# Attention queries stored head by head in full 128-row tiles with zeros, in a two-block float32 model kernel

## The reference

```python
# block 1, heads of 64
h = rms_norm(x, mix_norm_g);  proj = h @ w_in          # 1024 x 8708
# four mixers, 4 heads each: stick breaking (sb), dilated (dil, 3 groups), forgetting (fox), differential (diff)
sb:   z = q k^T / 8, log-sigmoids and a suffix sum over keys, then exp, times v
dil:  s_g = q_g k_g^T / 8 - slope * distance, softmax over the 3 groups together, times v_g
fox:  softmax(q k^T / 8 + cum_q - cum_k), times v
diff: w = softmax(q_0 k_0^T / sqrt(32) - slope*dist) - lam * softmax(q_1 k_1^T / sqrt(32) - slope*dist), w v
      # q_0, q_1, k_0, k_1: two halves of 32 of one head of 64
x = x + (sum_n sigmoid(gate_n) * (y_n @ w_branch_n)) @ w_out
x = x + relu(rms_norm(x) @ w_up)**2 @ w_down;  x = rms_norm(x, final_norm_g)
# block 2: 8 heads of 64 with q/k norm and rotary (one block of 256 keys, so plain causal attention),
# beside a gated causal convolution of 31 taps with a layer norm; then w_out, then a gated MLP
```

## Time and profile before

| what | value |
|---|---|
| median of 3 runs | 833.12 us (832.48 to 836.74) |
| the profiled execution: its time, its span | 833.48 us, 831.6 us |
| PE busy | 801.0 us, 96% of the span |
| PEld, DVE, ACT, POOL busy | 659.9, 470.7, 405.2, 34.6 us |
| share of PE in the chain that ended last | 85% |
| granted TensorE clock | 0.999 of full speed |
| HBM read | 134.43 MB, 163 GB/s over the span |

### The profile page before, as it was taken

One profiled execution on the slowest core, in us unless ns is written; L12 is line 12 of the kernel. 1 busy time (PEld: TensorE's weight loads), 2 busy tenths in 40 slices (PEclk: granted clock), 3 DMA queues, 4 the chain that ended last, 5 costly groups with the idle time before them and its releaser, 6 DMA issues.

```text
span 831.6 us, 9701 instructions
## 1 busy us (share of the span) xinstructions
PE 801.0 (96%) x3930; PEld 659.9 (79%) x3930; DVE 470.7 (57%) x616; ACT 405.2 (49%) x539; POOL 34.6 (4%) x33
## 2 busy tenths in 40 slices
PE   5999999999999999999999999898999999999997
PEld 4877888877778778788888877776887788888896
DVE  5454444556666767544544536688965745445443
ACT  5555444445555744654454454745446544343340
POOL 0000000000001320000000003011000000000000
PEclk9999999999999999999999999999999999999999
DMA  9832333343445445655555562935113655545341
GB/s 341 290 131 99 126 102 133 121 152 107 148 153 177 156 141 204 217 203 173 180 196 167 194 202 72 384 109 202 52 51 102 238 168 198 193 166 201 101 153 50
DMA packets 68268, 136.25 MB, mean 164 GB/s; under 512 B 2304, under 2 KB 7040, under 8 KB 67584
## 3 DMA queue, kind: packets, MB, share of 16 engines
q1 hardware_dynamic: 67760, 134.44, 47.3%
q10 hardware_dynamic: 464, 1.20, 0.4%
HBM read 134.43 MB, written 1.05 MB: 163 GB/s over the span
## 4 chain that ended last, share of the span: by engine, by line
PE 85%; DVE 7%; ACT 3%; issue 2%; DMA 1%; POOL 1%; ACTq 0%; SPq 0%; DVEq 0%
PE b L542 19%; PE b L544 18%; PE b L543 18%; PE SS L542 4%; PE SS L544 4%; PE SS L543 4%; PE TT L511 3%; DVE wlo L1407 3%; PE OO L542 2%; PE OO L544 2%; PE OO L543 2%; PE OO L850 2%; ACT whi L1009 1%; PE SS L627 1%; PE b L686 1%
## 5 line engine op out<-in xcount | busy, mean ns | idle before, releaser
L1407 DVE TENSOR_TENSOR wlo<-raw,whi 128x2048 fp32r<-128x2048 f32 (+2 forms) x123 | 273.8, 2228 | 169.4 <-ACT whi L1009 169.3
L1009 ACT CAST whi<-raw 128x2048 fp32r<-128x2048 f32 (+2 forms) x123 | 227.3, 1850 | 129.6 <-PE b L544 91.7
L542 PE MATMUL b<-whi,Ahi 128*128 128x512 f32 (+2 forms) x568 | 222.1, 391 | 5.2 <-DVE wlo L1404 2.9
L544 PE MATMUL b<-whi,Alo 128*128 128x512 f32 (+2 forms) x568 | 216.0, 380 | 0.0
L543 PE MATMUL b<-wlo,Ahi 128*128 128x512 f32 (+2 forms) x568 | 215.6, 380 | 0.0
L542 PEld LDWEIGHTS b<-whi,Ahi 128*128 128x128 f32 x568 | 107.6, 189 | 28.2 <-issue 4.8
L544 PEld LDWEIGHTS b<-whi,Alo 128*128 128x128 f32 x568 | 107.4, 189 | 20.9
L543 PEld LDWEIGHTS b<-wlo,Ahi 128*128 128x128 f32 x568 | 107.8, 190 | 18.3
L542 PE MATMUL b<-whi,Bhi 128*128 128x512 f32 x168 | 66.8, 398 | 2.7 <-DVE gates L1647 2.7
L544 PE MATMUL b<-whi,Blo 128*128 128x512 f32 x168 | 65.5, 390 | 0.0
L543 PE MATMUL b<-wlo,Bhi 128*128 128x512 f32 x168 | 65.5, 390 | 0.0
(11 more groups left out here) (264 smaller groups left out, 992.0 us busy)
## 6 DMA issues: line engine op xcount, KB each, us to landing
raw<-in_w_in SPq DMA_DIRECT2D x42, 1024.0 KB, 4.9
raw<-in_w_up SPq DMA_DIRECT2D x16, 1024.0 KB, 5.4
raw<-in_w_dn SPq DMA_DIRECT2D x16, 1024.0 KB, 5.0
raw<-in_w_d SPq DMA_DIRECT2D x11, 1024.0 KB, 4.9
raw<-in_w_g SPq DMA_DIRECT2D x10, 1024.0 KB, 5.0
raw<-in_w_u SPq DMA_DIRECT2D x10, 1024.0 KB, 5.0
raw<-in_w_out SPq DMA_DIRECT2D x8, 1024.0 KB, 5.0
raw<-in_w_br SPq DMA_DIRECT2D x4, 1024.0 KB, 5.0
```

The lines of the kernel that those rows point to most:

```text
L542: e.matmul(dst, xh, H[:, kc, c0:ce], start=first and kc == krs[0], stop=False)
L544: ins = e.matmul(dst, xl, H[:, kc, c0:ce], start=False, stop=last and kc == krs[-1])
L1009: e.copy(whi[:, s, 0:m], raw[:, r, 0:m]).then_inc(s_hi, 1)
L1407: e.tensor_tensor(wlo[:, s, 0:m], raw[:, r, 0:m], whi[:, s, 0:m].bitcast(F32), ALU.subtract).then_inc(s_lo, 1)
```

## The change

Each query head gets a tile of its own with all 128 rows: its 64 rows (32 for a diff half) hold the query and the others hold zeros. The keys stay packed two heads to a tile, and the score matmuls read all 128 rows of both, so that the zeros cancel the other head. This needs more query tiles, so tiles are reused: fox queries go over the sb queries, diff queries over the dil queries in `qkB`, and `KTILE` lists where the keys lie. The diff pair of chunk 8 is turned at slots 42 and 44 rather than 36 and 37. POOL writes the zeros: three memsets after its first root, one of `qkB` again when the last dil scores are done, and one of the query half of `qk2T` after block 1's last up product. A copy of query tiles becomes two copies of 64 rows, or four of 32 rows for diff (`qk_parts`); keys still take one. `s_zd` and its wait are gone. `qk2T` grows from 8 to 12 tiles and lies where `qkA` was.

```diff
-        s = 4 * c + (4 if first else 5)
+        s = 4 * c + (4 if first else 5) if c < 8 else 42 if first else 44
...
-    def qk_tile(i):
-        return qkA[:, i, :] if i < 16 else qkB[:, i - 16, :]
+    qB4 = qkB[:].rearrange("p (r a) q -> p r a q", r=2)
+    KTILE = {2: 8, 10: 4, 12: 6, 14: 10, 18: 8, 22: 4}
+    def qk_parts(dst):
+        if dst in KTILE:
+            return [(slice(0, 128), qkA[:, KTILE[dst]:KTILE[dst] + 2, :])]
+        if dst == 20:
+            return [(slice(32 * b, 32 * b + 32), qB4[32 * b:32 * b + 32, :, b, :]) for b in range(4)]
+        if dst in (4, 6):
+            return [(slice(64 * b, 64 * b + 64), qB4[64 * b:64 * b + 64, :, 2 * b + (dst - 4) // 2, :])
+                    for b in range(2)]
+        o = 12 if dst == 8 else 0
+        return [(slice(64 * b, 64 * b + 64), qkA[64 * b:64 * b + 64, o + 2 * b:o + 2 * b + 2, :]) for b in range(2)]
...
-            p = 64 * (h % 2)
-            Q, K = qkA[p:p + 64, h // 2, :], qkA[p:p + 64, 2 + h // 2, :]
+            Q, K = qkA[:, 2 * (h % 2) + h // 2, :], qkA[:, 8 + h // 2, :]
...
-                    q, k = 4 + 2 * g + h // 2, 10 + 2 * g + h // 2
-                    ins = e.matmul(SS[:, m * g:m * g + m], qkA[p:p + 64, q, qs], qkA[p:p + 64, k, 0:m],
-                                   start=True, stop=True)
+                    q = qkB[:, 4 * pr + 2 * a + g, qs] if g < 2 else qkA[:, 12 + 2 * a + pr, qs]
+                    ins = e.matmul(SS[:, m * g:m * g + m], q, qkA[:, (4, 6, 10)[g] + pr, 0:m], start=True, stop=True)
...
-                e.matmul(Z[:, 0:m], qkB[p:p + 64, h // 2, qs], qkB[p:p + 64, 2 + h // 2, 0:m], start=True, stop=False)
+                e.matmul(Z[:, 0:m], qkA[:, 2 * a + pr, qs], qkA[:, 8 + pr, 0:m], start=True, stop=False)
...
-                e.matmul(Z[:, 0:m], qkB[p:p + 32, 4 + h // 2, qs], qkB[p:p + 32, 6 + h // 2, 0:m],
-                         start=True, stop=True).then_inc(s_zd, 1)
-                w.wait_ge(s_zd, n - 15)
-                e.matmul(Z[:, m:2 * m], qkB[p + 32:p + 64, 4 + h // 2, qs], qkB[p + 32:p + 64, 6 + h // 2, 0:m],
-                         start=True, stop=True).then_inc(s_z, 1)
+                for c in range(2):
+                    ins = e.matmul(Z[:, m * c:m * c + m], qkB[:, 4 * pr + 2 * a + c, qs], qkA[:, 4 + pr, 0:m],
+                                   start=True, stop=True)
+                ins.then_inc(s_z, 1)
...
-            p = 64 * (h % 2)
-            Z, q, k = bank[bk], qk2T[p:p + 64, h // 2, :], qk2T[p:p + 64, 4 + h // 2, :]
+            Z, q, k = bank[bk], qk2T[:, 4 * (h % 2) + h // 2, :], qk2T[:, 8 + h // 2, :]
...
-            e.mul(q, src, sc).then_inc(s_tpa, 1)
+            w.wait_ge(s_qz, 1)
+            for rows, q in qk_parts(dst):
+                ins = e.mul(q, src[rows], sc)
+            ins.then_inc(s_tpa, 1)
...
-            e.mul(qk2T[:, 4 * qk:4 * qk + 4, 128 * t:128 * t + 128], bank[5].rearrange("p (k q) -> p k q", k=4),
-                  0.125 if qk == 0 else 1.0).then_inc(s_q2, 1)
+            if qk:
+                e.copy(qk2T[:, 8:12, ts], src).then_inc(s_q2, 1)
+                return
+            w.wait_ge(s_qz, 3)
+            e.mul(qk2T[0:64, 0:4, ts], src[0:64], 0.125)
+            e.mul(qk2T[64:128, 4:8, ts], src[64:128], 0.125).then_inc(s_q2, 1)
...
-            q = qkA[:, dst:dst + 2, :] if dst < 16 else qkB[:, dst - 16:dst - 14, :]
-            e.tensor_scalar(q, bank[5].rearrange("p (j q) -> p j q", j=2), sc, None, ALU.mult).then_inc(s_tpd, 1)
+            w.wait_ge(s_qz, 2 if dst == 20 else 1)
+            for rows, q in qk_parts(dst):
+                ins = e.tensor_scalar(q, src[rows], sc, None, ALU.mult)
+            ins.then_inc(s_tpd, 1)
...
         root("r1", r1_, r1v, 2)
+        for o in (0, 12):
+            e.memset(qkA[:, o:o + 4, :], 0.0)
+        e.memset(qkB[:], 0.0).then_inc(s_qz, 1)
+        w.wait_ge(s_z, 8)
+        e.memset(qkB[:], 0.0).then_inc(s_qz, 1)
...
+        w.wait_ge(s_mm, done("up", 7, 1, 1))
+        e.memset(qk2T[:, 0:8, :], 0.0).then_inc(s_qz, 1)
```

More of the change, by code:

```diff
@@ L182, in build @@
         qkA = sb("qkA", [128, 16, S], c=r1)
+    with ExitStack() as r1:
+        qk2T = sb("qk2T", [128, 12, S], c=r1)
     with ExitStack() as r2:
@@ L210, in build @@
         g2 = ExitStack()
-        qk2T = sb("qk2T", [128, 8, S], c=g2)
         par2 = sb("par2", [128, 1024 + 128 + 256], c=g2)
@@ L238, in build @@
     s_sz, s_sc, s_spv = sem("s_sb_scores"), sem("s_sb_sums"), sem("s_sb_pv")
-    s_z, s_zd, s_t, s_o, s_fc = sem("s_scores"), sem("s_scores_half"), sem("s_pturn"), sem("s_pv"), sem("s_fsum")
+    s_z, s_t, s_o, s_fc = sem("s_scores"), sem("s_pturn"), sem("s_pv"), sem("s_fsum")
     s_ut, s_rt, s_cp = sem("s_uturn"), sem("s_rturn"), sem("s_convpe")
@@ L259, in build @@
     s_dve = sem("s_dve_step")
-    s_rs, s_pm, s_pg, s_pad = [sem(n) for n in ("s_rsqrt", "s_mixadd", "s_gfin", "s_pad")]
+    s_rs, s_pm, s_pg, s_pad, s_qz = [sem(n) for n in ("s_rsqrt", "s_mixadd", "s_gfin", "s_pad", "s_qzero")]
     s_pool = sem("s_pool_step")
@@ L616, in z @@
             qs = slice(128 * qb, 128 * qb + 128)
-            p = 64 * (h % 2)
+            pr, a = h // 2, h % 2
             if kind == "dil":
@@ L1045, in evac @@
             if c >= 10:
-                w.wait_ge(s_tp, 12)
+                if c >= 12:
+                    w.wait_ge(s_tp, 12)
                 o = gates[:, t, 512 * (c - 10):512 * (c - 10) + 512]
@@ L1269, in r2 @@
             w.wait_ge(s_rt, i + 1)
-            e.mul(qk2T[:, 4 * qk:4 * qk + 4, 128 * t:128 * t + 128], bank[5].rearrange("p (k q) -> p k q", k=4),
-                  0.125 if qk == 0 else 1.0).then_inc(s_q2, 1)
+            src = bank[5].rearrange("p (k q) -> p k q", k=4)
+            ts = slice(128 * t, 128 * t + 128)
+            if qk:
[4 more added lines that the diff above has]
+            e.mul(qk2T[64:128, 4:8, ts], src[64:128], 0.125).then_inc(s_q2, 1)
         def phases():
@@ L1469, in te @@
             w.wait_ge(s_tp, i + 1)
-            q = qkA[:, dst:dst + 2, :] if dst < 16 else qkB[:, dst - 16:dst - 14, :]
-            e.tensor_scalar(q, bank[5].rearrange("p (j q) -> p j q", j=2), sc, None, ALU.mult).then_inc(s_tpd, 1)
+            src = bank[5].rearrange("p (j q) -> p j q", j=2)
+            w.wait_ge(s_qz, 2 if dst == 20 else 1)
+            for rows, q in qk_parts(dst):
+                ins = e.tensor_scalar(q, src[rows], sc, None, ALU.mult)
+            ins.then_inc(s_tpd, 1)
         def sm(h):
```

## The result

The changed kernel takes 823.59 us (median of 4 runs, 822.13 to 824.13) against 833.35 us before (4 runs on the same occasions, 832.48 to 836.74): a ratio of 0.9872, 95% interval 0.9854 to 0.9889, 1.3% faster. The profiled execution takes 823.72 us, 9.8 less than before, with a span of 821.9, 9.7 less. The forecast was 819.7 in a range of 815.5 to 824: the direction, the main mechanism and the range held; 3.9 us of the forecast gain did not come.

A forecast was written before the change was run, and what follows sets the result against it. PE, busy 96% of the span, was taken as the bound. Terms 9.6 + 1.65 - 0.5 + 2.65 = 13.4 us off 833.48 gave 820.1, or 819.7 as the median, range 815.5 to 824.

The forecast's parts named there:

- Height costs 0.2 us at each change, both ways: Block 1's score matmuls: 48 switches between short and 128-row matmuls cost PE 0.20 us each; removing them saves 9.6 us.
- `s_zd` and slot 36: Block 1: dropping the wait between diff halves saves 1.65 us over four pairs; the bank wait at slot 36 goes, 1.26 saved.
- The loop of block 2 becomes DVE's: Block 2's attention loop: without 6.4 us of switches on PE, DVE at 3.44 us a head becomes the bound; 2.65 us gained.
- Rival (a): Block 2's loop: DVE keeps up, so all PE switches pay, 6.4 us instead of 2.65; time 816.0, chance 0.09.
- Slot 28 "grows by 0.61: a loss": Block 1, fox queries: their copy becomes two, so PE's wait for the bank grows by 0.61 us.
- Zeros on POOL, "hidden": POOL's three groups of zeros: the first done in time, the second and third hidden behind other work; no cost.
- Extra copies, "I take 0": Query copies on DVE and ACT, both blocks: delays of 0.6 us or less each, covered by 5 us in hand; cost 0.
- Slots 43 and 45: Diff turns' new places: four copies lose about 0.1 us at slot 43, a copy behind ACT's cast 1.05 at 45.
- rival (b): Bank hand-overs at slots 28, 43, 45 cost 2.5 us each, or extra copies 4 to 6; 824 to 826, chance 0.09.
- (c): Score matmuls: the 0.2 us belongs to reading `qkA` or the semaphore wait, not height; 1.2 us remain, 832, chance 0.05.
- (d): Start of block 1: POOL's first zeros come 22.6 us late, stalling PE; slower, 837.3 us and more, chance 0.03.

The follow-up runs named there:

- experiment 1: Changed kernel, but block 1's sb, dil and fox score matmuls read only the 64 rows of their own head; 831.74 us, ratio 0.9975 to the kernel before.
- experiment 2: Changed kernel, but block 2's attention scores read only the 64 rows of their own head; 827.18 us, ratio 0.991 to the kernel before.
- experiment 7: Changed kernel, with seven convolution taps moved ahead of block 2's loop and six instead of seven per head in it; 822.69 us, ratio 0.9851.
- experiment 4: Changed kernel, but POOL's second memset waits for one score task more (slot 40 instead of 38); 824.74 us, ratio 0.9881 to the kernel before.
- experiment 5: Changed kernel, but the diff keys are turned at slot 43 instead of 44; 820.74 us, ratio 0.9828 to the kernel before.
- experiment 6: Changed kernel, but in block 2 the norm's squares stand ahead of ACT's query copies, and sums ahead of other DVE work; 824.04 us, ratio 0.9868.
- experiment 8: Kernel before, with only the copy of the turned fox queries (slot 28) done as two copies of 64 rows; 837.66 us, ratio 1.0047.
- experiment 3: Changed kernel, but the fox queries are turned at slot 29 instead of 28; 822.21 us, ratio 0.9851 to the kernel before.
- experiment 9: Changed kernel with five shifts together: fox queries, POOL's second zeros, diff keys, squares ahead of copies, seven taps; 817.18 us, ratio 0.9795.
- experiment 10: Kernel of experiment 9, with chunk 3's two key pairs turned at slots 18 and 19 instead of 16 and 17; 813.34 us, ratio 0.9751.

## Why the prediction was right, and what it missed

*Height costs 0.2 us at each change, both ways.* Right, and shown by experiment 1, which puts back height and nothing else: 7.3 us for 40 switches. The term measured 9.2 for 9.6, a switch being 0.19 rather than 0.20. Of the 48, 8 lie in the diff pairs, where their share is reckoned and not tested.

*`s_zd` and slot 36.* Right in size (1.6 and 1.26). That full tiles give up matmuls side by side made no loss, as the sum had it.

*The loop of block 2 becomes DVE's.* Right, by experiments 2 and 7, though PE needs 2.77 us and more a head and not 2.65, and waits only once, at the end. It gained 3.15 us for 2.65: I read DVE as gapless at 3.44 us a head, but without PE's switches it needs 3.36, so it had stood 0.08 us a head for PE, below what the rows show as a gap. Rival (a), 816, falls.

*Slot 28 "grows by 0.61: a loss".* The wait grew by 0.70 and was foreseen; its size as a cost was not. **The step that failed is that a microsecond of PE's waiting costs a microsecond.** Behind 1.77 us of waiting the granted clock was 0.50 until 117, which made 2.3 us out of the additional 0.7. Of the eight traces with this longer wait (the changed kernel, experiments 1, 2 and 4 to 8) six have the low clock behind it, and the four without it (before, 3, 9, 10) have none there; experiment 8 has nothing of the change but the longer copy. So the wait is what opens the way to it, and whether it comes in a given execution is chance as far as these runs show: the 2.3 us could have been 0.7.

*Zeros on POOL, "hidden".* The memsets were early enough at all three places (1.81 us for 2048 columns, 0.9 ns each, for my bound of 2.5), but I had asked only whether POOL would be late, and whether weight splits had room. The trace of before had DVE's splits undisturbed beside POOL's additions; its `nlf` writes, one input from SBUF and one output, are stopped by a memset, and they stand in a chain with little to spare: they took 1.4 us longer, of which 0.8 reached PE, shown by experiment 4.

*Extra copies, "I take 0".* True in block 1, where splits have 5 us in hand. Wrong in block 2: the copy stood ahead of the squares, and their chain ends in a wait of PE. I had looked at the cover of the splits and not at this chain. 0.6 us, shown by experiment 6.

*Slots 43 and 45.* Mechanisms right, sizes 0.5 for 0.1 and 1.3 for 1.05. Four copies in a row start 0.69 to 0.70 apart, not 0.61: the 0.61 was the distance to an instruction of another kind. The end of the copy at slot 45 was also added up 0.04 too late (180.22 and 0.6 are 180.82).

So rival (b), copies in the place of switches, took part: 4.7 us of losses at banks and copies instead of 1.8, 1.6 of it by the clock. Rivals (c) and (d) did not come.

Open: why the clock falls at one wait in some executions and not in others with the same wait. This holds for slot 28 (6 of 8 traces), for the block boundary (waits of 1.74 and 2.1 us; 5 of 12), for the rotated keys (2.65 to 3.25 us; 5 of 12) and for the end of the loop (1.63 us; once, in experiment 1). In the traces of before and of the changed kernel it stayed up at boundary and keys; in those of experiments 1, 3 and 9 it fell at both. The scatter of one kernel's times goes with it: over the 31 executions of the kernel before that were timed beside the experiments, the 15 with a mean granted clock of 0.998 or 0.999 took 832.8 to 833.8 us, and of the 16 with 0.994 or 0.995 all but one (833.25) took 834.8 to 836.5. At which wait it fell in those not profiled, no row shows.

## What to carry to other kernels

In a stream that PE fills, read the distance between ends of neighbouring matmuls: it shows costs that neither busy time nor idle time has, such as the 0.17 to 0.2 us here for every change between 64-row and 128-row matmuls. A handful of short matmuls between full ones was dearer here than the same with zeros in it, as long as making the zeros and the additional copies stays off every bank hand-over, so price these by what waits for them, chain by chain. And look first at the longest waits of PE, which can cost their own length and a low clock behind: five small shifts in the lists and a sixth in experiment 10, three of them hand-overs of a bank moved by a slot or two, gave the second half of the 20 us.

## What the runs showed of the hardware that was not expected

- A wait of 1.77 us on PE, behind dense work, was followed by half clock from 113.6 to 117.0 (experiment 8: from 115 to about 122), in six of the eight traces with that wait. The low clock added 1.6 us in the changed kernel, and in experiment 8 some 3. From 40 to 800 us, the twelve traces (before, after and the ten experiments) have 17 falls, each beginning in or within 1.4 us behind a wait of PE of 1.62 us or more. They have some 50 waits of that length, so two in three were harmless. No fall follows any of the 46 waits of 1.0 to 1.45 us.
- A POOL memset of 2048 columns (1.81 us) stops DVE's `TENSOR_SCALAR` from SBUF to SBUF: two of them took 1.91 us instead of 0.48. A `TENSOR_TENSOR` of DVE with two SBUF inputs (the split at 20.04) took its usual 2.29 us beside the same memset at 20.18. The Trainium skill, "GPSIMD Engine Reference", section 1, names contention with DVE instructions in a two-port mode or with two SBUF inputs; here one with a single SBUF input is stopped. Whether it runs in such a mode no row shows.
- Copies of fewer rows take as long as those of 128: 0.69 us for 512 columns on DVE with 128, 64 or 32 rows, and 0.58 to 0.59 on ACT with 128 or 64.
